# Hybrid decoder step on one core: norm scales applied at evacuations, router scaled by token, sample attention in column tiles

## The chip, the core and the metric

The kernel runs on one core of a Trainium2 chip. The metric is device time in microseconds; lower is better. Engines: TensorE (PE), VectorE (DVE), ScalarE (ACT), GpSimd (POOL) and the DMA queues that SyncE (SP) and GpSimd issue to. The engines run their own instruction queues in order and wait for each other on semaphores.

## What is computed

One step of a two-layer decoder for 264 tokens: 256 of a prompt, and 8 of a sample group with 256 past positions each. Width 1024, all in float32. Cut to what matters:

```
h = rmsnorm(x, norm_mix[0]);  z = gelu(h @ w_in);  u, v = split(z);  v = layernorm(v)
x = x + (u * (W_s v + b)) @ w_out                    # chunked mixer
h = rmsnorm(x, norm_ffn[0]);  x = x + (silu(h @ wg) * (h @ wu)) @ wd
kv = rmsnorm(x, kv_norm) @ w_kv;  h = rmsnorm(x, norm_mix[1])
q, gates = h @ b_w_in;  x = x + (gated compressed + selected + window attention) @ b_w_out
h = rmsnorm(x, norm_ffn[1]);  x = x + top-2-of-8 expert SwiGLU(h)
y = rmsnorm(x, norm_final)
```

rmsnorm(x, g) is x * rsqrt(mean(x * x) + eps) * g for each token.

## The kernel before, in words

Activations lie transposed: channels on partitions (8 chunks of 128, `KC`), the 264 tokens (`NT`) along the free axis. To keep float32 accuracy, each operand is split in two fp32r halves: ACT casts it (`_hi`), DVE subtracts the cast from the original (`_lo`, the rest), and PE adds up hi*hi, hi*lo and lo*hi. One **item** is 128 output columns of a dense weight; its product (`product`, L1370) is 24 matmuls of 264 columns into one of four banks `B[0..3]` (18 for the last part of the down stage). Items come in the stages vu (16), ao (8), gu (44), dn (24), kv (12), q (8), bo (8). SP loads four items as a 2 MB tile of a two-slot ring (L434); ACT casts (`round_to`, L568, L576), DVE takes the rest (`rest_to`, L892, L897), into three buffers `d_hi`, `d_lo`. The order of each engine's queue is written out by hand: `round_to(stage, c)` and `rest_to(stage, c)` run up to two items ahead of product c, and they stand between the other work of that engine.

A norm before: ACT squares x (L564, L587), DVE adds the chunks up (`add_up`, L858), PE multiplies by a matrix of 1/1024 (`mean_of`, L1362), ACT takes the root (`std`, L557, with a table load), DVE the reciprocal (`inv_std`, L853). Only then `split_normed` (L877, L883, L887) and `round_normed` (L579) scale and split x, chunk by chunk, and the products of the next stage start. Evacuations: gelu, silu, the copy to `kvT` and half of `Q` on ACT (L596, L600, L631, L645, L652), products and residual additions on DVE (L982, L958), other half of `Q` on DVE (L1011). In the kv stage DVE also copies the new keys to `X2` (L1001), while POOL clears `Q` (L492 to L494). The mask of the mixer's matrix is applied by DVE (L912).

Sample attention: `sample_scores` (L1504) adds 16 matmuls of 256 columns into one bank for each of two key sets, with queries `Qz` zero outside their sample's rows (L1509). The values are 32 matmuls with 16 output rows, one sample each (L1594); their rows are copied out (L717, L1130) and turned back by 16 small matmuls (L1605). Then follow the 16 heads of the prompt: scores, softmax, turning, weighing.

Router: norm of x, `normed(late("ffn1"))` (L1156), 8 matmuls (L1625), a copy (L740), transposes of tokens and logits (L1631, L1636), then a chain of small DVE operations (L1174 on). POOL zeroes `slot_rows` and `out_rows` in DRAM (L481 to L484) and scatters token rows there. Eight expert blocks follow in this execution (L1690 on). SP loads their first 11 MB as soon as the heads are done.

Of the kernel before, what the change touches and what calls it, by code (L numbers as in the profile page):

```python
# [21 lines left out]
F32 = mybir.dt.float32  # L22
# [6 lines left out]
P = 128  # L29
# [104 lines left out]
def build(nc, xT, wd, moe, vectors, params, late_in, spatial, spatial_bias, consts, cmp_pages, k_pages, v_pages, win_k, win_v, state_win, page_table,  # L134
          y_out, v_out, kv_out, past_out):
    with ExitStack() as ctx:
# [15 lines left out]
        zeros = sb("zeros", [P, 256])  # L152

# [36 lines left out]
        win_v_past = sbd("win_v_past", [P, SLOT])  # L190
        sq3 = slc_v[:, 0:KC * NT].rearrange("p (k t) -> p k t", t=NT)
# [21 lines left out]
        b_s = carve(8, NT)  # L213

# [5 lines left out]
        orow = arena[0:NH, qz_at:qz_at + NS * 2 * P]  # L220
# [86 lines left out]
        x_in = sem("x_in")  # L307
# [49 lines left out]
        zeros_ready, rows_zeroed, slots_ready, early_ready = sem("zeros_ready"), sem("rows_zeroed"), sem("slots_ready"), sem("early_ready")  # L357
        sel_ready, tok_zero = sem("sel_ready"), sem("tok_zero")
# [44 lines left out]
        def _(sp):  # L403
            sp.dma_start(x[:], xT).then_inc(x_in, 16)
            sp.dma_start(VE[:], vectors).then_inc(setup_in, 16)
            wn = 0
# [4 lines left out]
            for n, t in enumerate(TILES):  # L411
# [21 lines left out]
                else:  # L433
                    sp.dma_start(ring[:, n % NSLOT, :], wd[wn]).then_inc(done, 16)  # L434
# [31 lines left out]
            for half in range(2):  # L466
                sp.wait_ge(h_ready, 44 + 4 * half)
                sp.dma_start(y_out[:, 4 * half:4 * half + 4, :], hB[:, 4 * half:4 * half + 4, :]).then_inc(y_stored, 16)
# [6 lines left out]
        def _(pool):  # L475
            nc.gpsimd.memset(zeros[:], 0.0).then_inc(zeros_ready, 1)
            pool.wait_ge(vn_ready, 8)
            pool.dma_start(v_out, vT).then_inc(v_stored, 16)
            pool.dma_start(past_out, state_win).then_inc(past_stored, 16)
            pool.wait_ge(zeros_ready, 1)  # L480
            for rows in (slot_rows.rearrange("b p n -> (b p n)"), out_rows[0:NO_ROW, :].rearrange("r n -> (r n)")):  # L481
                rows = rows.rearrange("(p q n) -> p q n", p=P, n=256)
                pool.dma_start(rows, zeros[:].unsqueeze(1).to_broadcast(list(rows.shape))).then_inc(rows_zeroed, 16)
            pool.dma_start(out_rows[NO_ROW:NO_ROW + 1, :].rearrange("o (q n) -> (o q) n", n=256), zeros[0:4, :]).then_inc(rows_zeroed, 16)  # L484
# [22 lines left out]
            pool.dma_start(grow[:], gsam[0:NS, :]).then_inc(grow_in, 16)  # L507

# [39 lines left out]
        def _(act):  # L548
# [8 lines left out]
            def std(n, eps):  # L557

                act.wait_ge(mean_done, n)
                nc.scalar.activation(rstd[:, :], STAT[:, 0:NT], ACT.Sqrt, bias=vector("eps")[:, eps:eps + 1]).then_inc(std_ready, 1)  # L560

            def squares(norm, k, dst=hB):
# [1304 lines left out]
```

## Time and profile before

| | us |
|---|---|
| three runs | 1375.67, 1376.95, 1380.04 |
| median | 1376.95 |
| the profiled execution, device time | 1382.43 |
| its span | 1380.8 |
| PE busy / DVE / ACT / POOL | 1306.5 / 1055.2 / 920.7 / 73.0 |

The profile is of one execution. The dense stages end near 388 us, the sample attention near 468, the heads near 546, the output projection at 570, the routing near 595; the expert blocks last to 1363. Matmuls are pipelined, so the duration of one is longer than its step to the next.

### The profile page before, as it was taken

How to read it: one execution, taken by the hardware profiler on the slowest of the kernel's cores; microseconds unless marked ns; L12 is line 12 of the kernel's file. 1: busy time of each engine (PE TensorE's matmuls, PEld its weight loads, DVE VectorE, ACT ScalarE, POOL GpSimd, SP SyncE). 2: the span in 40 equal slices, each digit the busy share in tenths (PEclk: the TensorE clock that was granted, in tenths of full speed). 3: DMA queues.
4: the chain of work that ended last, by engine and by line, in shares of the span. 5: the costliest groups of instructions: out<-in, count | busy, mean ns of one | idle time of the engine just before them, and what ended most of it. 6: DMA issues, size and time to landing. Idle time of an engine off the chain costs nothing.

```text
span 1380.8 us, 21526 instructions
## 1 busy us (share of the span) xinstructions
PE 1306.5 (95%) x7292; PEld 1109.1 (80%) x7292; DVE 1055.2 (76%) x1539; ACT 920.7 (67%) x1353; POOL 73.0 (5%) x74
## 2 busy tenths in 40 slices
PE   4998999996998999899999999999999999999996
PEld 4988999996966677678888888888788888887874
DVE  5776555458423487689899899898998998998985
ACT  5535444445372287478798788887987987887863
POOL 0010000004200000020000000000000000002500
PEclk9999999998998999999999999999999999999998
DMA  8399544455565001679999899899998998998930
GB/s 328 130 379 402 187 180 181 177 197 175 187 218 187 1 1 48 288 299 421 363 392 409 318 419 396 332 417 370 352 413 326 404 406 323 416 394 320 408 146 32
DMA packets 59280, 391.50 MB, mean 284 GB/s; under 512 B 6639, under 2 KB 12915, under 8 KB 20627
## 3 DMA queue, kind: packets, MB, share of 16 engines
q1 hardware_dynamic: 50578, 354.29, 65.2%
q0 software_dynamic: 8640, 36.40, 7.2%
q8 instruction: 38, 0.62, 0.2%
q14 instruction: 24, 0.19, 0.0%
HBM read 367.41 MB, written 27.45 MB: 286 GB/s over the span
## 4 chain that ended last, share of the span: by engine, by line
PE 84%; DVE 9%; ACT 3%; issue 3%; DMA 0%; ACTq 0%; DVEq 0%
PE bank L1710 16%; PE bank L1712 16%; PE bank L1711 16%; PE bank L1381 8%; PE bank L1382 8%; PE bank L1383 8%; DVE w_lo L1263 2%; PE bank L1695 1%; PE bank L1509 1%; PE bank L1594 1%; PE bank L1567 1%; ACT w_hi L756 1%; DVE rstd L856 1%; ACT arena L662 1%; PE bank L1555 1%
## 5 line engine op out<-in xcount | busy, mean ns | idle before, releaser
L1263 DVE TENSOR_TENSOR w_lo<-raw,w_hi 128x1024 fp32r<-128x1024 f32 x528 | 623.2, 1218 | 37.1 <-ACT w_hi L756 19.7
L756 ACT CAST w_hi<-raw 128x1024 fp32r<-128x1024 f32 x528 | 543.0, 1055 | 95.3 <-PE bank L1712 94.4
L1710 PE MATMUL bank<-w_hi,xg_hi 128*128 128x512 f32 x704 | 275.2, 391 | 1.4 <-DVE w_lo L1263 1.4
L1712 PE MATMUL bank<-w_hi,xg_lo 128*128 128x512 f32 x704 | 274.3, 390 | 0.0
L1711 PE MATMUL bank<-w_lo,xg_hi 128*128 128x512 f32 x704 | 273.9, 389 | 0.0
L897 DVE TENSOR_TENSOR d_lo<-ring,d_hi 128x1024 fp32r<-128x1024 f32 x120 | 146.6, 1223 | 102.6 <-ACT d_hi L576 102.4
L1381 PE MATMUL bank<-hA_hi,d_hi 128*128 128x264 f32 x640 | 187.9, 294 | 21.1 <-DVE hA_lo L887 15.2
L1382 PE MATMUL bank<-hA_lo,d_hi 128*128 128x264 f32 x640 | 185.3, 289 | 0.0
L1383 PE MATMUL bank<-hA_hi,d_lo 128*128 128x264 f32 x640 | 184.9, 289 | 0.0
L576 ACT CAST d_hi<-ring 128x1024 fp32r<-128x1024 f32 x120 | 125.4, 1046 | 58.5 <-PE bank L1383 55.0
L1710 PEld LDWEIGHTS bank<-w_hi,xg_hi 128*128 128x128 f32 x704 | 132.3, 188 | 29.3 <-DVE w_lo L1263 2.1
L1712 PEld LDWEIGHTS bank<-w_hi,xg_lo 128*128 128x128 f32 x704 | 132.1, 188 | 27.8
L1711 PEld LDWEIGHTS bank<-w_lo,xg_hi 128*128 128x128 f32 x704 | 132.2, 188 | 27.3
L1710 PE MATMUL bank<-w_hi,hm_hi 128*128 128x512 f32 x352 | 148.2, 421 | 1.9 <-DVE w_lo L1263 0.6
L1381 PEld LDWEIGHTS bank<-hA_hi,d_hi 128*128 128x128 f32 x640 | 123.9, 194 | 23.7 <-issue 20.6
L1712 PE MATMUL bank<-w_hi,hm_lo 128*128 128x512 f32 x352 | 139.4, 396 | 0.0
L1711 PE MATMUL bank<-w_lo,hm_hi 128*128 128x512 f32 x352 | 138.5, 393 | 0.0
L1382 PEld LDWEIGHTS bank<-hA_lo,d_hi 128*128 128x128 f32 x640 | 124.8, 195 | 0.1
L1383 PEld LDWEIGHTS bank<-hA_hi,d_lo 128*128 128x128 f32 x640 | 124.0, 194 | 0.0
L1710 PEld LDWEIGHTS bank<-w_hi,hm_hi 128*128 128x128 f32 x352 | 66.6, 189 | 19.5 <-DVE w_lo L1263 8.5
L1712 PEld LDWEIGHTS bank<-w_hi,hm_lo 128*128 128x128 f32 x352 | 66.6, 189 | 15.9
L1711 PEld LDWEIGHTS bank<-w_lo,hm_hi 128*128 128x128 f32 x352 | 67.1, 191 | 11.6
(320 smaller groups left out, 1611.0 us busy)
## 6 DMA issues: line engine op xcount, KB each, us to landing
raw<-in_moe SPq DMA_DIRECT2D x264, 1024.0 KB, 6.8
ring<-in_wd SPq DMA_DIRECT2D x30, 2048.0 KB, 8.5
out_rows<-zeros POOLq DMA_DIRECT2D x1, 6656.0 KB, 62.1
slot_rows<-zeros POOLq DMA_DIRECT2D x1, 6144.0 KB, 44.9
out_rows<-yrow POOLq DMA_DIRECT2D x8, 512.0 KB, 7.8
xs<-slot_rows POOLq DMA_DIRECT2D x7, 512.0 KB, 3.6
arena<-in_cmp_pages POOLq DMA_DIRECT2D x16, 128.0 KB, 2.5
X2v<-in_cmp_pages POOLq DMA_DIRECT2D x16, 128.0 KB, 2.8
```

Source lines behind the costliest of these rows:

```text
L576: nc.scalar.copy(d_hi[:, n % NDS, :], raw_item(n)).then_inc(d_hi_ready, 1)
L662: nc.scalar.copy(lines[:, n % NLINE, :], X2[v][:, m:8 * SEGS:8]).then_inc(line_ready, 1)
L756: nc.scalar.copy(w_hi[:, i % NSPLIT, :], raw[:, u % NRAW, ITEM * (i % 2):ITEM * (i % 2) + ITEM])\
L856: settle(V.reciprocal(rstd[:, :], rstd[:, :]))
L897: V.tensor_tensor(d_lo[:, n % NDS, :], raw_item(n), d_hi[:, n % NDS, :].bitcast(F32), ALU.subtract)\
L1263: V.tensor_tensor(w_lo[:, i % NSPLIT, :], raw[:, (i // 2) % NRAW, ITEM * (i % 2):ITEM * (i % 2) + ITEM], w_hi[:, i % NSPLIT, :].bitcast(F3 ...
L1381: T.matmul(out, w_hi_[:, j, :], hi[:, k, :], start=(first and j == 0), stop=False)
L1382: T.matmul(out, w_hi_[:, j, :], lo[:, k, :], start=False, stop=False)
L1383: i = T.matmul(out, w_lo_[:, j, :], hi[:, k, :], start=False, stop=(last and k == ks[-1]))
L1710: T.matmul(out, lhs_hi, hi, start=first, stop=False)
L1711: T.matmul(out, lhs_hi, lo, start=False, stop=False)
L1712: return T.matmul(out, lhs_lo, hi, start=False, stop=last)
```

## The change

The token scale of a norm is no longer applied to x. ACT rounds x times the norm's weight (`round_weighted`) as each chunk of x is ready, DVE takes its rest, the products start at once, and the reciprocal root multiplies each product at its evacuation, on DVE (`scaled`, `u_scale`, the gate, up and query scalings). ACT then applies gelu and silu in SBUF. Means stand one or two products into the next stage; `root_table` loads the root's table ahead of time. At the start SP loads vectors, one item and x in halves:

```diff
-            sp.dma_start(x[:], xT).then_inc(x_in, 16)
             sp.dma_start(VE[:], vectors).then_inc(setup_in, 16)
+            sp.dma_start(ring[:, 0, 0:DITEM], wd[0][:, 0:DITEM]).then_inc(item_in[0], 16)
+            for half in range(2):
+                sp.dma_start(x[:, 4 * half:4 * half + 4, :], xT[:, 4 * half:4 * half + 4, :]).then_inc(x_in[half], 16)
+            sp.wait_ge(item_in[0], 16)
+            sp.dma_start(ring[:, 0, DITEM:2 * DITEM], wd[0][:, DITEM:2 * DITEM]).then_inc(item_in[1], 16)
...
+                    first = 2 * DITEM if n == 0 else 0
+                    sp.dma_start(ring[:, n % NSLOT, first:], wd[wn][:, first:]).then_inc(done, 16)
```

POOL applies the mask of the mixer, and zeroes the DRAM rows only after the gates are stored:

```diff
+            pool.wait_ge(spatial_in, 48)
+            nc.gpsimd.tensor_tensor(wsT[:], w_s, const("upto").unsqueeze(1).to_broadcast([P, 8, P]), ALU.mult).then_inc(ws_ready, 1)
+            nc.gpsimd.tensor_tensor(dg[0:NS], ident[0:NS, 0:NS].unsqueeze(1).to_broadcast([NS, 8, NS]),
+                                    vector("w00")[0:NS, :].unsqueeze(2).to_broadcast([NS, 8, NS]), ALU.mult).then_inc(ws_ready, 1)
...
+            pool.wait_ge(zeros_ready, 1)
+            for rows in (slot_rows.rearrange("b p n -> (b p n)"), out_rows[0:NO_ROW, :].rearrange("r n -> (r n)")):
+                rows = rows.rearrange("(p q n) -> p q n", p=P, n=256)
+                pool.dma_start(rows, zeros[:].unsqueeze(1).to_broadcast(list(rows.shape))).then_inc(rows_zeroed, 16)
```

ACT (in the kv stage it also copies the new keys, `new_keys`, after item 7 and at the start of q):

```diff
+            def root_table():
+
+                nc.scalar.activation(warm[0:1, 0:1], zeros[0:1, 0:1], ACT.Sqrt)
...
+            def round_weighted(weight, k, dst, ready):
+
+                nc.scalar.activation(dst[:, k, :], x[:, k, :], ACT.Copy, scale=weight[:, k:k + 1]).then_inc(ready, 1)
...
+            act.wait_ge(zeros_ready, 1)
+            root_table()
+            act.wait_ge(setup_in, 16)
+            round_to("vu", -2)
             for k in range(KC):
-                nc.scalar.activation(hB[:, k, :], x[:, k, :], ACT.Square).then_inc(sq_ready, 1)
-            act.wait_ge(setup_in, 16)
+                if k % 4 == 0:
+                    act.wait_ge(x_in[k // 4], 16)
+                round_weighted(vector("mix0"), k, hA_hi, h_hi_ready)
+            round_to("vu", -1)
...
+                nc.scalar.activation(sqr[:, k, :], x[:, k, :], ACT.Square).then_inc(sq_ready, 1)
+            round_to("vu", 1)
             std(1, 0)
...
-                projected(act, "vu", c)
-                nc.scalar.activation(vT[:, c, :], B[c % 4][:, 0:NT], ACT.Gelu_apprx_tanh).then_inc(v_ready, 1)
+                act.wait_ge(v_scaled, c + 1)
+                nc.scalar.activation(vT[:, c, :], vT[:, c, :], ACT.Gelu_apprx_tanh).then_inc(v_ready, 1)
...
+                if c == 3:
+                    std(3, 1, ln_rstd)
...
+                    for k in range(KC):
+                        act.wait_ge(ln_scaled, k + 1)
+                        nc.scalar.activation(vT[:, k, :], vT[:, k, :], ACT.Identity, bias=vector("lnb")[:, k:k + 1]).then_inc(vn_ready, 1)
...
+            root_table()
             for c in range(KC):
                 round_to("ao", c)
+                act.wait_ge(x_ready, c + 1)
+                round_weighted(vector("ffn0"), c, hA_hi, h_hi_ready)
                 squares(1, c)
+            round_to("gu", 1)
             std(4, 0)
...
-                nc.scalar.activation(sil[:, f % 2, :], B[2 * (f % 2)][:, 0:NT], ACT.Silu).then_inc(sil_ready, 1)
+                act.wait_ge(gate_scaled, f + 1)
+                nc.scalar.activation(sil[:, f % 2, :], sil[:, f % 2, :], ACT.Silu).then_inc(sil_ready, 1)
...
                 round_to("dn", 12 * (c // 4) + 8 + c % 4)
+                act.wait_ge(x_ready, KC + c + 1)
+                round_weighted(vector("kvn"), c, hA_hi, h_hi_ready)
...
+                round_weighted(vector("mix1"), c, hC_hi, q_hi_ready)
...
+                if c < KC:
+                    round_weighted(vector("mix1"), c, hB, gate_in)
+                if c == 7:
+                    new_keys(0)
...
+                if c == 0:
+                    projected(act, "kv", 11)
+                    new_keys(1)
+            act.wait_ge(gp_scaled, 1)
+            nc.scalar.activation(gT[0:48, :], gT[0:48, :], ACT.Sigmoid, bias=par("bgate")[0:48, :]).then_inc(sig_ready, 1)
...
+            act.wait_ge(orow_done, 1)
+            nc.scalar.copy(orow[:, :], B[0][:, :]).then_inc(orow_ready, 1)
...
+            root_table()
             for c in range(KC):
                 round_to("bo", c)
+                act.wait_ge(x_ready, 16 + c + 1)
+                nc.scalar.activation(hB[:, c, :], x[:, c, :], ACT.Copy, scale=late("ffn1")[:, c:c + 1]).then_inc(weighted, 1)
...
+            act.wait_ge(mean_done, 6)
+            nc.scalar.activation(tok_rstd[:, 0:2], STAT[:, 0:2], ACT.Sqrt, bias=vector("eps")[:, 0:1])
```

DVE (its copies of new keys, `split_normed`, the mask, and the copies of value rows are gone):

```diff
+            def rest_weighted(weight, k, hi, lo, which):
...
+                dve.wait_ge(hi_done, nrest[which])
+                V.scalar_tensor_tensor(lo[:, k, :], x[:, k, :], weight[:, k:k + 1], hi[:, k, :].bitcast(F32), ALU.mult, ALU.subtract)\
+                    .then_inc(lo_done, 1)
...
+            dve.wait_ge(setup_in, 16)
+            rest_to("vu", -2)
             for k in range(KC):
-                add_up(hB, k, sq_ready, k + 1)
-            dve.wait_ge(setup_in, 16)
+                rest_weighted(vector("mix0"), k, hA_hi, hA_lo, 0)
+            rest_to("vu", -1)
+            for k in range(KC):
+                add_up(sqr, k, sq_ready, k + 1)
+            rest_to("vu", 1)
...
+            def scaled(to, stage, c, ready):
+                projected(dve, stage, c)
+                V.tensor_tensor(to, B[c % 4][:, 0:NT], rstd[:, :], ALU.mult).then_inc(ready, 1)
...
-                add_up(vT, k, v_ready, k + 1)
+                scaled(vT[:, k, :], "vu", k, v_scaled)
+                if k:
+                    add_up(vT, k - 1, v_ready, k)
+            add_up(vT, KC - 1, v_ready, KC)
...
+            u_scale(0)
+            u_scale(1)
...
+                if k == 4:
+                    u_scale(2)
...
+            u_scale(3)
+            rest_to("vu", 11)
+            inv_std(ln_rstd)
             for k in range(KC):
                 if k == 5:
...
+                    u_scale(4)
+                V.scalar_tensor_tensor(vT[:, k, :], vT[:, k, :], vector("lng")[:, k:k + 1], ln_rstd[:, :], ALU.mult, ALU.mult)\
...
+            rest_to("vu", 13)
+            u_scale(5)
+            u_scale(6)
+            u_scale(7)
...
+                for r in rests:
+                    rest_weighted(vector(r[0]), c, *r[1:])
...
+                if f >= 2:
+                    dve.wait_ge(hF_ready, f - 1)
+                V.tensor_tensor(sil[:, f % 2, :], B[2 * (f % 2)][:, 0:NT], rstd[:, :], ALU.mult).then_inc(gate_scaled, 1)
...
+                V.tensor_tensor(hB[:, f % 4, :], B[2 * (f % 2) + 1][:, 0:NT], rstd[:, :], ALU.mult).then_inc(up_scaled, 1)
...
+            for c in range(12):
+                rest_to("kv", c)
+                scaled(kvT[:, c, :], "kv", c, kv_ready)
...
+                for odd, done in ((0, q_even), (1, q_odd)):
+                    rows = slice(64 * odd, 64 * odd + 64)
+                    V.scalar_tensor_tensor(Q[half:half + 64, 2 * c + odd, :], B[c % 4][rows, 0:NT], HD ** -0.5, rstd[rows, :],
+                                           ALU.mult, ALU.mult).then_inc(done, 1)
...
+                i = V.scalar_tensor_tensor(col(0, t)[0:r, :], MISC[0:r, 8 * t:8 * t + 8], tok_rstd[0:r, t:t + 1], b_router[0:r, :],
+                                           ALU.mult, ALU.add)
```

PE (sample scores and values in four column tiles; each group of 32 rows holds two samples; router matmuls between the output products; the mean there is one column per token group):

```diff
+                    pe.wait_ge(v_scaled, c - 3)
...
+                    pe.wait_ge(u_scaled, c - 11)
                 product(B[c % 4], hA_hi, hA_lo, each=chunks_of(h_ready, 0) if c == 0 else None)
+                if c == 1:
+                    mean_of()
                 if c == 8:
                     mean_of()
-                if c == 12:
+                if c == 11:
...
+                if f == 0:
+                    mean_of()
...
                 if c < 4:
-                    pe.wait_ge(x_ready, 16)
+                    pe.wait_ge(x_ready, 13 + c)
...
+                if c == 1:
+                    mean_of()
+            pe.wait_ge(q_lo_ready, 8)
+            pe.wait_ge(gate_in, 8)
...
-                for j in range(16):
-                    i = T.matmul(B[n][:, 0:PAST], Qz[:, j % 2, j // 2, :], keys[:, j // 2, j % 2, :], start=(j == 0), stop=(j == 15))
+                for j in range(4):
+                    for g in range(4):
+                        b, rows_ = 2 * g + j // 2, slice(32 * g, 32 * g + 32)
+                        i = T.matmul(B[n][rows_, 0:PAST], Qz[:, j % 2, b, rows_], keys[:, b, j % 2, :], start=(j == 0), stop=(j == 3))
...
-            for b in range(NS):
-                out = B[b // 2][0:NH, 256 * (b % 2):256 * (b % 2) + 256]
+            for half in range(2):
                 for j in range(4):
-                    i = T.matmul(out, PTs[:, j, b * NH:(b + 1) * NH], vals[j // 2][:, b, j % 2, :], start=(j == 0), stop=(j == 3))
-                if b % 2:
-                    i.then_inc(orow_done, 1)
+                    for g in range(4):
+                        rows_ = slice(32 * g, 32 * g + 32)
+                        i = T.matmul(B[0][rows_, 256 * half:256 * half + 256], PTs[:, j, rows_], vals[j // 2][:, 2 * g + half, j % 2, :],
+                                     start=(j == 0), stop=(j == 3))
+            i.then_inc(orow_done, 1)
...
+                    pe.wait_ge(orow_ready, 1)
+                for half in range(2):
+                    T.matmul(by_half(rows_, half), orow[:, 256 * half + c * P:256 * half + c * P + P], by_half(ident, half),
...
+                if c >= 2:
+                    logits(c - 2)
+            logits(KC - 2)
+            logits(KC - 1)
...
+            turn_tokens(0, 0)
+            pe.wait_ge(sum_step, 42)
             for t, (a, z) in enumerate(spans):
+                i = T.matmul(STAT[0:z - a, t:t + 1], total[:, a:z], mean[:, 0:1], start=True, stop=True)
+            i.then_inc(mean_done, 1)
+            nmean[0] += 1
+            pe.wait_ge(lT_ready, 1)
```

## Rows read from the trace of the kernel before

**Rows 1.** Page: the chain that ended last, by engine.

```profile
PE 84%; DVE 9%; ACT 3%; issue 3%; DMA 0%; ACTq 0%; DVEq 0%
```

**Rows 2.** Busy time by stretch: length; PE, PEld, DVE, ACT, POOL; clock, DMA share, GB/s.

```profile
390.00:470.00 80.00, 73.96 (x326) 50.98 (x327) 18.49 (x69) 30.43 (x57) 0.64 (x1) 0.86 0.40 140
470.00:546.00 76.00, 73.32 (x477) 56.90 (x476) 62.51 (x247) 60.45 (x224) 0.00 (x0) 0.99 0.01 1
...
780.00:1250.00 470.00, 469.05 (x2122) 382.90 (x2121) 427.64 (x449) 388.47 (x469) 4.83 (x9) 1.00 0.95 378
```

**Rows 3.** Instruction groups by line; busy, mean ns, then idle before and its releaser.

```profile
L897 DVE TENSOR_TENSOR d_lo<-ring,d_hi 128x1024 fp32r<-128x1024 f32 x120 | 146.6, 1223 | 102.6 <-ACT d_hi L576 102.4
...
L576 ACT CAST d_hi<-ring 128x1024 fp32r<-128x1024 f32 x120 | 125.4, 1046 | 58.5 <-PE bank L1383 55.0 <-DMA ring<-in_wd 3.4
...
L958 DVE TENSOR_TENSOR x<-x,bank 128x264 f32<-128x264 f32 x24 | 10.3, 429 | 25.1 <-PE bank L1383 25.1
```

**Rows 4.** Chain in order of time, start: start us, us, what.

```profile
0.98 5.09 DMA x<-in_x
...
13.92 1.81 DVE rstd L856
...
18.68 0.56 PE bank L1381
```

**Rows 5.** Timeline, seams up to gate/up: start us, us, what, idle before and releaser.

```profile
71.13 1.06 PE L1411 MATMUL bank<-consts_sb,arena 128*128 128x128 f32 x8 [0.33 <-DVE arena L937]
...
105.58 0.43 DVE L958 TENSOR_TENSOR x<-x,bank 128x264 f32<-128x264 f32 x1 [0.99 <-PE bank L1383]
...
108.48 0.43 DVE L958 TENSOR_TENSOR x<-x,bank 128x264 f32<-128x264 f32 x1 [0.85 <-PE bank L1383]
...
123.71 0.43 DVE L982 TENSOR_TENSOR hB<-sil,bank 128x264 f32<-128x264 f32 x1 [0.32 <-PE bank L1383]
```

**Rows 6.** Timeline, down to key/value.

```profile
310.73 0.43 DVE L958 TENSOR_TENSOR x<-x,bank 128x264 f32<-128x264 f32 x1 [0.28 <-PE bank L1383]
...
330.09 5.98 DVE L1001 COPY arena<-arena 64x128 f32<-64x128 f32 x1
...
340.90 0.38 ACT L645 COPY arena<-bank 128x264 f32<-128x264 f32 x1 [2.98 <-PE bank L1383]
```

**Rows 7.** Timeline, PE ahead of the compression products.

```profile
390.52 0.53 PE L1473 MATMUL bank<-consts_sb,arena 48*128 48x48 f32 x3 [2.27 <-ACT arena L654]
...
393.68 1.91 PE L1489 MATMUL bank<-arena,params_sb 128*128 128x512 f32 x2
...
398.62 1.04 PE L1489 MATMUL bank<-arena,params_sb 128*128 128x512 f32 x2
```

**Rows 8.** Chain, sample attention.

```profile
414.72 7.10 PE bank L1509 x32
424.41 8.78 PE bank L1509 x32
...
445.60 15.28 PE bank L1594 x64
...
467.36 0.61 PE bank L1607 x2
```

**Rows 9.** Timeline, DVE at the router.

```profile
570.19 0.43 DVE L958 TENSOR_TENSOR x<-x,bank 128x264 f32<-128x264 f32 x1 [1.55 <-PE bank L1383]
...
581.69 0.17 DVE L1174 TENSOR_TENSOR lg<-bank,late_sb 128x16 f32<-128x16 f32 x1 [2.15 <-PE bank L1636]
```

**Rows 10.** Timeline, SP issues the last of the value loads.

```profile
413.81 0.43 SPq L432 DMA_DIRECT2D win_v_past<-in_win_v  x1
```

**Rows 11.** Page: DMA issues; KB each, median us from issue to landing.

```profile
ring<-in_wd SPq DMA_DIRECT2D x30, 2048.0 KB, 8.5
out_rows<-zeros POOLq DMA_DIRECT2D x1, 6656.0 KB, 62.1
```

**Rows 12.** DMA issues from 60 to 140 us.

```profile
ring<-in_wd SPq DMA_DIRECT2D x5, 2048.0 KB, 11.1
```

More of the change, by code:

```diff
@@ L555, in settle, with std, squares @@
                 act.wait_ge(act_step, nstep[0])
[L557 removed]
+            def std(n, eps, dst=rstd):
                 act.wait_ge(mean_done, n)
[L560 to L562 removed]
+                nc.scalar.activation(dst[:, :], STAT[:, 0:NT], ACT.Sqrt, bias=vector("eps")[:, eps:eps + 1]).then_inc(std_ready, 1)
+            def squares(norm, k, dst=sqr):
                 act.wait_ge(x_ready, 8 * norm + k - 7)
@@ L571, in round_to @@
                     n = rounded[0]
-                    if n % 4 == 0:
+                    if n < 2:
+                        act.wait_ge(item_in[n], 16)
+                    elif n == 2 or n % 4 == 0:
                         arrived(act, WTILES[n // 4])
@@ L714, in _ @@
             exp_head(1)
-            for j in (0, 2):
-                act.wait_ge(orow_done, j + 1)
-                nc.scalar.copy(orow[:, 512 * j:512 * j + 512], B[j][0:NH, :]).then_inc(orow_ready, 1)
+            act.wait_ge(orow_done, 1)
+            nc.scalar.copy(orow[:, :], B[0][:, :]).then_inc(orow_ready, 1)
             for h in range(NH):
@@ L746, in _ @@
                     act.wait_ge(ht_done, 2 * t + half + 1)
-                    nc.scalar.copy(htok[0:r, t, 512 * half:512 * half + 512], HT[2 * t + half][0:r, :]).then_inc(ht_ready, 1)
+                    nc.scalar.activation(htok[0:r, t, 512 * half:512 * half + 512], HT[2 * t + half][0:r, :], ACT.Copy,
+                                         scale=tok_rstd[0:r, t:t + 1]).then_inc(ht_ready, 1)
             act.wait_ge(rank_in, 1)
@@ L953, in _, with add_chunk @@
                         .then_inc(gated_lo, 1)
-            def add_chunk(c, norm, stage, item, squared=hB):
+            def add_chunk(c, norm, stage, item, squared=sqr, rests=()):
                 rest_to(stage, item - 1)
@@ L1446, in _ @@
                             pe.wait_ge(hF_lo_ready, ks[-1] + 1)
-                        if part == 0 and half == 0 and j < 2:
-                            pe.wait_ge(hF_ready, FC)
+                        if part == 0 and half == 0:
+                            pe.wait_ge(hF_ready, FC - 1 if j < 2 else FC)
                         product(B[j], hF_hi, hF_lo, ks, part == 0, part == 2)
-            mean_of()
             for c in range(12):
                 if c < 4:
-                    pe.wait_ge(x_ready, 16)
+                    pe.wait_ge(x_ready, 13 + c)
                 if c >= 4:
@@ L1602, in _ @@
                 if c == 0:
-                    pe.wait_ge(orow_ready, 4)
-                for b in range(NS):
-                    T.matmul(rows_[:, b * NH:(b + 1) * NH], orow[:, 256 * b + c * P:256 * b + c * P + P], ident[0:NH, 0:NH],
+                    pe.wait_ge(orow_ready, 1)
+                for half in range(2):
+                    T.matmul(by_half(rows_, half), orow[:, 256 * half + c * P:256 * half + c * P + P], by_half(ident, half),
                              start=False, stop=False, skip_group_check=True)
@@ L1615, in _, with logits @@
             weigh(NH - 1)
+            def logits(k):
+                pe.wait_ge(weighted, k + 1)
+                i = T.matmul(MISC[0:NE, 0:NT], w_router[:, k, :], hB[:, k, :], start=(k == 0), stop=(k == KC - 1))
+                if k == KC - 1:
+                    i.then_inc(lT_done, 1)
             for c in range(KC):
```

191 lines of the change are left out of this document (78 added, 113 removed).

## The prediction

> **What bounds the kernel now.** I read the chain of waits first: it lies 84% on TensorE (PE) and 9% on VectorE (DVE) [rows 1]. Then the busy time by stretch [rows 2]: in the expert blocks PE is busy 469.05 of 470 us at full clock. The change leaves their code alone, so I take nothing from them. From 390 to 470 us the mean granted clock is only 0.86: part of that stretch runs at 1.2 instead of 2.4 GHz. So the change can act at four places: the start, the seams between dense stages, the sample attention, and the router. I price each on the profiled execution (span 1380.8 us, device time 1382.43). The median of the runs shown is 1376.95, 5.48 below it, and I subtract the same gain from the median.
>
> **Prices.** A 1024-column cast on ScalarE (ACT) takes 1.05 us, its rest on DVE 1.22, a 264-column DVE operation that reads a bank 0.43 [rows 3]. The trace has no scaling at an evacuation; the last of these is the nearest row, and I take it for each new scaling and each weighted rounding or rest (bounds 0.35, what back-to-back ones leave, and 0.6). Back to back, operations start some 0.07 earlier than their durations say.
>
> **Start and first projection.** Now x lands at 6.07, the reciprocal takes 1.81 from 13.92, and the first product starts at 18.68 [rows 4]. After: vectors, one weight item and half of x (1.1 MB together, like x alone now) land near 6.3, so the product starts near 7.8, 11 us earlier. It is not kept. Squares, mean, root and reciprocal now follow the second product (ending near 16, its chunks at 1.2 GHz at first), so the first scaling comes at 20 and the fifth product near 23. From there a loop is formed: scaling on DVE, gelu on ACT, ACT's next cast, DVE's next rest, next scaling. Its steps 0.36 + 0.31 + 0.97 + 1.14, with some 0.2 of handovers, are 3.0 us against the 2.90 at which PE takes a product, from the addition to x at 105.58 to the one at 108.48 [rows 5]. In the LayerNorm more DVE and ACT work stands ahead of the rests: u scalings between sums, and the bias additions, now on ACT, ahead of the cast for the last product. Following the three queues step by step I get PE waits of 1.4, 1.9, 1.1, 1.5 and 2.6 us, 8.5 together. The mask moved to GpSimd frees 1.2 us on DVE, but may hold DVE's two-input rests. The v transposes start near 70 instead of 71.13 [rows 5]: gain 1, bounds -4 (all waits longer by half) and +5 (half of them absent).
>
> **Output projection to gate/up.** Now the last x addition starts at 108.48, and the second gate/up product ends just before 123.71 [rows 5]. That is 15.2 us, of which two products are 5.8. After, the split of x is made chunk by chunk beside the products (0.43 more on ACT and on DVE of 2.90 us, covered). Only a mean of 0.33 stands between the two products, and root and reciprocal hide behind the next ones, since four banks are free. Gain 9.1. Per gate/up pair DVE rises from about 3.3 to 4.2 us of 5.8: still covered. The start of the down product no longer waits for the last multiply: 0.9, less 0.4 of new waits in the short down items (two weighted rests per chunk): 0.5.
>
> **Down to key/value.** The last addition starts at 310.73, the fifth product of the stage ends at 340.90 [rows 6]: 30.2 us, with two splits in the gap and one DVE copy of 5.98 us beside a GpSimd memset. After: five products of 2.90, a mean, 0.5 waiting at the first and 1.7 at the second product (rests queued behind x additions), together 17.1. The eight copies per half move to ACT (0.25 each, in its 1.4 us of slack per item). Gain 13.1.
>
> **Before the attention.** PE waits 2.27 us for the sigmoid and its table load, then runs its first line product in 1.91 us for two records, later pairs in 1.04 [rows 7]. The sigmoid goes ahead of the last query product, three line copies are ready, and PE has no gap before them: gain 2.3 + 1.8 = 4.1.
>
> **Sample attention in column tiles.** Scores: 32 records in 7.10 us, and 32 in 8.78 (its beginning at half clock). Values: 64 records in 15.28 us at 16 output columns, 0.239 a record, no cheaper than 128 columns at 0.222 [rows 8]. So time follows the 256 streamed columns, and a record leaves most of the array unused; the count of streams is unchanged. Bounds: serial, gain 0; four groups fully side by side, a quarter. I take a third, near the quarter, since the rows show the array's width idle. Scores: 4.7, and 4.3 at the half clock, which I let stand: 9.0. Values: 5.6, some of it at 1.2 GHz, instead of 15.3: 9.7. The Trainium skill (TensorE: Matmul & The Clock Gate, Measured speedup vs the span model) reports 2.38 times for three column tiles; at that efficiency four would give 3.2 times and a sum 0.6 us larger; no row here shows tiles. The part behind the values ends at 467.97 [rows 8], 7.1 us after them: sixteen turning matmuls become four, and the one bank copy hides behind the two matmuls ahead of them. With 12 records of some 0.22 and the copy's hand-over 7.1 becomes 3.4: gain 3.7 in either case.
>
> **Router.** The last x addition starts at 570.19, and DVE reads the logits at 581.69 [rows 9]: 11.5 us for mean, table load, root, reciprocal, eight weightings and eight router matmuls in a row. After: six router matmuls lie inside the output products (12 records of 0.22, +2.7 there), the table is loaded early, and the root is of three columns. What is left is an estimate from like rows: addition 0.4, weighting and square 0.8, sum 0.4, one-column means 0.7, roots 0.4, reciprocals 0.3, route transposes 0.4, hand-overs 0.5, together 3.9. 11.5 becomes 6.6; ACT's scaled token copies delay the exponential by 0.2 at the end: gain 4.7.
>
> **Sum:** 1 + 9.1 + 0.5 + 13.1 + 4.1 + 9.0 + 9.7 + 3.7 + 4.7 = 54.9. 1382.43 becomes 1327.5; the median 1376.95 becomes 1322.
>
> **Rivals.** (a) The column tiles run one after another. For: nothing in this trace shows two matmul streams overlapping, and at 16 columns none did (all in one column group). The gain falls by 18.7 to 36.2: 1341. The skill has the reason on the same page (What overlaps and what doesn't): weights are loaded beside running matmuls only if row groups differ, and these tiles share theirs. The trace does not bear that out for whole-array loads: PE is busy 469.05 of 470 us with a load before every matmul, all in one row group [rows 2].
> (b) The zeroing of the slot and output rows (6.6 and 6.1 MB) moves from 72 us to about 392, into the loads of the value pages, the last of which is issued at 413.81 [rows 10] and lands near 422. Now the zeroing lands after 62.1 us beside weight loads [rows 11], and ring loads of 2 MB, 8.5 us at the median, take 11.1 in that stretch [rows 11, 12]. If value loads lose half their rate, they land near 452, 20 us after PE now wants them (432); if they lose a third and SP's issue stays the limit, nothing waits. Middle: 12 us lost, 1334.
> (c) Slower: with PE mostly idle in the shortened sample part, the clock stays at 1.2 GHz through the 16 heads, where it is 0.99 now and PE is busy 73.3 of 76 us [rows 2]. A head, 76 us by 16 or 4.8 us, would take up to 4.8 more; from 12 heads on the gain is gone, and with all 16 it is 1399. Against: after the present half-clock stretch the full clock comes back before the heads.
> (d) The change does not do what it says at the first projection: GpSimd's mask multiply holds DVE's rests. The Trainium skill (SBUF — State Buffer, Who interferes with whom) says that a DVE instruction with two SBUF inputs contends with a GpSimd instruction that reads SBUF; no row of this trace has such a pair. The multiply happens once and costs one such multiply, 2 to 5 us: 1326, inside the forecast's range.
>
> **Numbers.** Chances: forecast with (d) 0.67, (a) 0.18, (b) 0.11, (c) 0.04. The forecast's own range is 1313 to 1331, from the bounds of the first projection (5 down, 4 up), full side-by-side streams (2.5) and the clock. The range given reaches to (a) and (b): 1312 to 1343. A difference under 0.3% (4.1 us) cannot be told from no change. Only (c), or several misses at once, reaches that: faster 0.95, same 0.02, slower 0.03.
>
> **What would show it.** First dense product near 8 us, v transposes near 70; no PE gap over 1 us before the gate/up stage; key/value seam 13 us shorter; table load for the sigmoid ahead of the last query product; records of different column groups starting under 0.1 us apart in the sample scores; logits on DVE about 6.6 us after the last output product; expert blocks unchanged. PE waiting for value pages would show (b), a clock under 0.9 in the heads (c). I am wrong if the seams keep waits, or if the first projection takes longer by more than its start gains.

## The result, and the profile after

The changed kernel takes 1343.22 us (median of four runs, 1341.46 to 1346.57), the kernel before 1377.87 in the same comparison: ratio 0.9749, interval 0.973 to 0.9768. The gain is 34.7 us, clearly a gain, but the forecast was 54.9 (1322), and the result lies just outside its range (1312 to 1343). The profiled execution took 1342.47 us, span 1340.7.

First the chain that ended last, by engine (page). Against [rows 1] PE falls from 84% to 76%. SyncE's issuing (SPq) and DMAs, which held nothing, now hold 5%:

```profile
PE 76%; DVE 10%; issue 5%; ACT 4%; SPq 3%; DMA 2%; DVEq 0%; ACTq 0%
```

Busy time by stretch, columns as in [rows 2]. The heads lie from 433 to 511 us now and run at full clock, and the expert blocks are as busy as before:

```profile
390.00:470.00 80.00, 61.97 (x455) 46.14 (x453) 43.74 (x172) 39.09 (x145) 0.00 (x0) 0.89 0.58 232
434.00:511.00 77.00, 73.20 (x483) 56.54 (x482) 64.09 (x253) 60.68 (x225) 0.00 (x0) 1.00 0.02 6
780.00:1250.00 470.00, 468.42 (x2120) 382.62 (x2120) 428.62 (x463) 385.58 (x467) 22.85 (x14) 1.00 0.95 377
```

Instruction groups, as [rows 3]. The new scaling at an evacuation (L967) costs 0.43, as assumed; a weighted rounding (L605) 0.51 and its rest (L940) 0.49, a little more than the 0.43 assumed:

```profile
L950 DVE TENSOR_TENSOR d_lo<-ring,d_hi 128x1024 fp32r<-128x1024 f32 x120 | 146.0, 1223 | 88.0 <-ACT d_hi L596 87.9
...
L967 DVE TENSOR_TENSOR arena<-bank,rstd 128x264 f32<-128x264 f32 x28 | 11.6, 427 | 8.4 <-PE bank L1453 8.2
L605 ACT ACTIVATE hA_hi<-x,vectors_sb 128x264 fp32r<-128x264 f32 x24 | 11.6, 512 | 13.3 <-DVE x L1023 12.9 <-DMA x<-in_x 0.3
L940 DVE SCALAR_TENSOR_TENSOR hA_lo<-x,vectors_sb,hA_hi 128x264 fp32r<-128x264 f32 x24 | 11.1, 486 | 1.2 <-ACT hA_hi L605 1.2
```

Then the timeline at the places the forecast named (start, duration, what, idle before and its releaser). The v transposes start at 73.34; before they started at 71.13 [rows 5]. The second gate/up product and the fifth key/value product end near 117.0 and 321.2, where they ended before 123.7 and 340.9 [rows 5, 6]. PE waits 12.90 us for the window's values; the logits reach DVE 3.6 us after the last addition to x (537.94), not 11.5 [rows 9]:

```profile
73.34 1.04 PE L1481 MATMUL bank<-consts_sb,arena 128*128 128x128 f32 x8
...
321.25 0.43 DVE L967 TENSOR_TENSOR arena<-bank,rstd 128x264 f32<-128x264 f32 x1 [0.59 <-PE bank L1453]
...
372.25 0.60 PE L1557 MATMUL bank<-consts_sb,arena 128*8 128x128 f32 x4 [2.33 <-DVE arena L1099]
372.51 2.26 POOL L524 DMA_DIRECT2D slot_rows<-zeros  x1
...
374.02 2.00 PE L1566 MATMUL bank<-arena,params_sb 128*128 128x512 f32 x2
...
393.65 1.93 PE L1588 MATMUL bank<-ring,arena 128*32 128x256 f32 x32
...
401.57 0.87 SPq L445 DMA_DIRECT2D win_v_past<-in_win_v  x1
...
422.90 1.51 PE L1674 MATMUL bank<-slc_v,arena 128*32 128x256 f32 x12 [12.90 <-DMA win_v_past<-in_win_v]
...
541.53 0.48 DVE L1244 SCALAR_TENSOR_TENSOR lg<-bank,tok_rstd,late_sb 128x8 f32<-128x8 f32 x3
```

Laid stretch by stretch over the profile of before, the two traces give this account (us gained):

| stretch | forecast | traces |
|---|---|---|
| start to the v transposes | +1 | -2.2 |
| to the third gate/up product | 9.1 | 8.9 |
| gate/up and down | 0.5 | 0.1 |
| down to key/value | 13.1 | 12.9 |
| last query product to the first sample score | 4.1 | 1.4 |
| sample scores to the first value product | 9.0 | 1.7 |
| values | 9.7 | 9.1 |
| turning back | 3.7 | 3.5 |
| heads | 0 | 0.7 |
| output projection and routing | 4.7 | 2.4 |
| expert blocks and end | 0 | 1.7 |

That is 40.2 between two profiled executions. The one of before was 4.6 us above its median, the one of after 0.8 below; less these, 34.8 is left, the measured gain. Four rows miss by more than 2: the scores' (7.3), the start (3.2), the seam before the attention (2.7) and the router (2.3).

### The profile page after: what moved, and what is told of

The parts are those of the page before. It is cut to its first block, busy times and chain, and to the rows that moved or that the text cites. A ratio compares the mean times of both kernels' runs of the same rounds, so it can differ in the third digit from the quotient of the medians.

```text
span 1340.7 us, 21550 instructions
## 1 busy us (share of the span) xinstructions
PE 1272.4 (95%) x7272; PEld 1082.5 (81%) x7272; DVE 1053.5 (79%) x1552; ACT 929.6 (69%) x1378; POOL 76.0 (6%) x76
## 4 chain that ended last, share of the span: by engine, by line
PE 76%; DVE 10%; issue 5%; ACT 4%; SPq 3%; DMA 2%; DVEq 0%; ACTq 0%
PE bank L1809 16%; PE bank L1811 16%; PE bank L1810 16%; PE bank L1451 7%; PE bank L1452 6%; PE bank L1453 6%; DVE w_lo L1333 3%; SPq L422 2%; DMA win_v_past<-in_win_v 2%; DVE d_lo L950 2%; PE bank L1794 1%; PE bank L1646 1%; ACT w_hi L812 1%; ACT d_hi L596 1%; DMA ring<-in_wd 1%
## 5 line engine op out<-in xcount | busy, mean ns | idle before, releaser
L1452 PEld LDWEIGHTS bank<-hA_lo,d_hi 128*128 128x128 f32 x640 | 121.9, 191 | 0.1
L1453 PEld LDWEIGHTS bank<-hA_hi,d_lo 128*128 128x128 f32 x640 | 121.3, 190 | 0.0
L1810 PEld LDWEIGHTS bank<-w_lo,hm_hi 128*128 128x128 f32 x352 | 66.9, 190 | 11.5
```

What stands on the lines that cost most here:

```text
L1452: T.matmul(out, w_hi_[:, j, :], lo[:, k, :], start=False, stop=False)
L1453: i = T.matmul(out, w_lo_[:, j, :], hi[:, k, :], start=False, stop=(last and k == ks[-1]))
L1810: T.matmul(out, lhs_hi, lo, start=False, stop=False)
```

## The experiments

Theory A was formed on the DMA view of 340 to 480 us (KB each, median us to landing). A load of a value page takes 14.4 us and that of the window's values 21.2, beside 12.8 MB of zeroing. The second fence has the same two loads in the kernel before:

```profile
out_rows<-zeros POOLq DMA_DIRECT2D x1, 6656.0 KB, 60.5
slot_rows<-zeros POOLq DMA_DIRECT2D x1, 6144.0 KB, 29.5
...
slc_v<-in_v_pages SPq DMA_DIRECT2D x16, 128.0 KB, 14.4
win_v_past<-in_win_v SPq DMA_DIRECT2D x1, 2048.0 KB, 21.2
```

```profile
slc_v<-in_v_pages SPq DMA_DIRECT2D x16, 128.0 KB, 2.3
win_v_past<-in_win_v SPq DMA_DIRECT2D x1, 2048.0 KB, 8.5
```

The timeline adds that not only the flights got longer. SyncE now takes 25.7 us to issue the sixteen page loads, where it took 17.2, so the last load leaves some 8 us later. The DMA share, the mean busy share of the 16 DMA engines, is 1.01 from 376.5 to 400 us, where it was 0.69 in the kernel before (398 to 422): they were full. The issues in the changed kernel, then in the kernel before:

```profile
375.81 25.72 SPq L443 DMA_DIRECT2D slc_v<-in_v_pages  x16
```

```profile
396.53 17.24 SPq L430 DMA_DIRECT2D slc_v<-in_v_pages  x16
```

**1. Zeroing after the value loads.**

```diff
             pool.dma_start(grow[:], gsam[0:NS, :]).then_inc(grow_in, 16)
+            pool.wait_ge(past_v_in, 16 * (NS * PAGES + 1))
             pool.wait_ge(zeros_ready, 1)
```

> The changed kernel with one wait more: GpSimd issues the zeroing of the slot and output rows only when all value pages and the window's values have landed (near 410 us). Theory A (the zeroing takes the bandwidth of the value pages, which land at 422.9 although TensorE wants them at 413.3): the value products start near 413.5 instead of 422.9, run nearer to full clock (4 to 6 us instead of 6.2), 1331 us, a gain of 9.5 to 12. Rival B (the pages are late because SyncE issues them late and slowly; the last leaves at 400.1 in any case): the values still land after 418 us and the gain is under 5 us. Rival C: the zeroing, now beside the heads and ending near 475, delays the output projection's or the experts' weights and gives part back; then the wait ahead of the values is gone but the total stays above 1337.

1332.46 us, ratio 0.967 (0.9656 to 0.9683). The page loads are issued in 17.2 us again, the last load leaves at 392.90 in place of 401.57 and lands 8.8 us later. PE waits only for DVE's copies and starts the values at 414.56. The values still take 6.6 us, at clock 0.55, so this part of the expectation missed. Theory A holds. Rival B falls with its premise: SyncE issued late because of the zeroing itself. C falls too.

**2. Zeroing early, as before.** The five lines move back behind the store of `v_out`.

> The changed kernel with the zeroing put back where the kernel before has it, right behind the store of the mixer's values (near 67 us). Theory A: the same gain at the values as with the late zeroing, 9.5 to 12 us, but the zeroing now lies beside the weight loads of the output projection and gate/up stages, which have 1.5 us to spare per item: 0 to 2 us lost there; 1331 to 1334. Rival B: under 5 us gained.

1331.93 us, ratio 0.9666 (0.9652 to 0.9681): the same gain, with nothing lost beside the weight loads, though the ring loads from 60 to 140 us now take 12.4 us (8.3 in the changed kernel). The same two rows as above, in this kernel:

```profile
slc_v<-in_v_pages SPq DMA_DIRECT2D x16, 128.0 KB, 2.4
win_v_past<-in_win_v SPq DMA_DIRECT2D x1, 2048.0 KB, 8.7
```

The later experiments on the changed kernel stand on this one, called E below, where nothing else is said.

**3. The mask on VectorE.** On the changed kernel; the multiply moves from GpSimd's queue to DVE's, behind `u_scale(6)`.

> The changed kernel with the mask of the mixer's matrix multiplied by VectorE again, in its idle 4 us before the last u scaling, instead of by GpSimd at 24.7 us. Theory D (GpSimd's multiply holds VectorE: the first copying addition at 25.12 takes 2.30 us instead of 0.43): that addition takes 0.43, the sixth product starts 0.5 to 1.9 us earlier, and 0.5 to 1.9 us are gained in all: 1341.5 to 1342.7. Rival E (the wait at 27 us comes from the loop of scaling, gelu, cast and rest that fills after the first reciprocal, not from GpSimd): no difference.

1343.4 us, ratio 0.9748: no difference from the change. The mechanism is in the trace: in the changed kernel DVE's addition of two SBUF tiles starts at 25.12 and ends at 27.42, with GpSimd's multiply (24.71 to 27.13), while a scaling from a bank at 24.78 took its 0.42 beside it. Without the multiply the addition takes 0.42. So theory D is right in its place, where the sixth product's gap of 0.63 is gone, and too small to be measured in the whole. First the changed kernel, then experiment 3:

```profile
24.71 2.42 POOL L492 TENSOR_TENSOR arena<-arena,consts_sb 128x1024 f32<-128x1024 f32 x1 [23.42 <-DMA arena<-in_spatial_bias]
...
25.12 2.30 DVE L922 TENSOR_TENSOR total<-arena 128x264 f32<-128x264 f32 x1
```

```profile
25.24 0.42 DVE L918 TENSOR_TENSOR total<-arena 128x264 f32<-128x264 f32 x1
```

**4. Column tiles, one group after the other.** On the kernel of experiment 1, only the order of the loops:

```diff
-                for j in range(4):
-                    for g in range(4):
+                for g in range(4):
+                    for j in range(4):
```

> The kernel of the late zeroing with the same column tiles and the same number of matmuls, only in another order: all matmuls of one column group in a row, then the next group, in the scores and in the values. Theory F (streams of different column groups run side by side only if they stand next to each other in TensorE's queue): each score set goes from 1.93 to about 7.1 us, the values from 4 to 6 us to 14 or 15; 19 to 20 us more than the late zeroing, some of the first set's hidden by nothing: near 1350. Rival G (the width of a tile alone makes a matmul cheap, whatever its neighbours are): the same times as the late zeroing, within 1 us.

1341.24 us, ratio 0.9738 (0.9721 to 0.9755): 8.8 above experiment 1. Neither theory's sizes hold. Windows over the first score set (32 records and a few others) and the values (64):

```profile
395.70:400.40 4.70, 4.70 (x35) 2.53 (x35) 1.33 (x6) 2.03 (x2) 0.00 (x0) 1.00 1.02 364
420.20:428.40 8.20, 8.16 (x65) 4.57 (x65) 0.00 (x0) 1.35 (x8) 0.00 (x0) 1.00 1.02 407
```

A record costs 0.143 in the scores (4.59 by 32), where it was 0.222 with full width [rows 8] and is 0.060 with neighbours of other groups (1.93 by 32). The starts of the single records in the traces say why. Within one group they stand 0.216 us apart, as they do at full width, so a narrow record is no cheaper by itself and rival G is out. But the first record of the next group starts at 396.640, beside the fifth of the eight before it (396.635): two groups run side by side for half of their records. In experiment 1 the records of all four groups start within 0.02 us (393.645 to 393.665), and the next four 0.24 later. So the whole gain of the tiles comes from groups running side by side, and the order decides how many do: theory F is right in kind, and wrong only in leaving no overlap where two groups meet. In the values 8.16 us at full clock stand against 6.6 at half clock (3.7 at full clock in experiment 6): there the clock takes most of what the order gives.

From the first score to the last value the two traces differ by 5.2 us. Another 2.4 lie before the third product of the first stage, which the edit does not touch, so the 8.8 between the medians is not all the order's.

**5. The kernel before with column tiles alone.** The loops of scores, values and turning back, and one bank copy by ACT, from the change.

> The kernel before with one part of the change alone: the sample scores, the values and the turning back in column tiles (the zeroing stays early, as it is there). By the changed kernel's trace the two score sets should take 1.93 us each instead of 7.10 and 8.78, the values 5 to 6.2 at half clock instead of 15.3, the turning 3.5 instead of 7.1: 24 to 25 us in all, near 1353. Rival: part of it is given back, because TensorE, now idle for more of the stretch, works at 1.2 GHz in the transposes, scores and heads beside it: 18 to 21 us, 1356 to 1359.

1357.26 us, ratio 0.9849 (0.9834 to 0.9864): 20.6 us gained, the rival's 18 to 21, not 24 to 25. The half clock moved in as the rival said: the second score set took 2.9 us, the values 5.35 (from the chain of waits):

```profile
416.57 2.86 PE bank L1507 x32
...
433.57 5.35 PE bank L1593 x64
```

**6. Waits filled with matmuls** (on E):

```diff
+            def filler(n):
+                for _ in range(n):
+                    T.matmul(STAT[:, 0:256], ident, kvT[:, 0, 0:256], start=True, stop=True)
+            filler(6)
             pe.wait_ge(vp_ready, 3)
...
+            filler(6)
             pe.wait_ge(spt_ready, 1)
```

> The kernel of the early zeroing with six matmuls of 256 columns more, which nobody reads, in each of the two places where TensorE waits in the sample attention (for the maxima of the sample scores, 2.7 us, and for the copies of the turned probabilities, 2.8 us). Theory H (these idle stretches are what the granted clock falls after, and the half clock lengthens the turning, the first head's scores, the values and the turning back): clock 1.0 in them, values in 3.9 us instead of 5.05, 3 to 5 us gained, 1327 to 1329. Rival I (the clock falls by something else, or the added matmuls end later than the waits they fill): no gain, or 1 us lost.

1328.66 us, ratio 0.9641 (0.9625 to 0.9657), 3.3 us under E. The window over the values: 65 records in 3.7 us at clock 1.0. E needed 5.05 at 0.72, the changed kernel 6.2 at 0.59. One row each of this kernel, of E, and of the changed kernel (its wait, then its values):

```profile
412.20:416.00 3.80, 3.71 (x65) 2.09 (x66) 0.03 (x1) 1.44 (x8) 0.00 (x0) 1.00 0.01 4
```

```profile
413.30:418.40 5.10, 5.05 (x65) 2.44 (x65) 0.00 (x0) 1.37 (x8) 0.00 (x0) 0.72 0.01 3
```

```profile
414.00:422.90 8.90, 0.00 (x1) 0.03 (x2) 0.00 (x0) 0.53 (x4) 0.00 (x0) 0.52 1.03 431
422.90:429.10 6.20, 6.20 (x65) 3.20 (x66) 0.00 (x0) 0.00 (x0) 0.00 (x0) 0.59 1.01 425
```

Theory H holds for this stretch. The two intervals overlap slightly, but from the first score to the last value the traces differ by 3.4 us, about as much as the medians. The clock has a share of chance too: at the first line products, ahead of any filling, it fell in E (371.8) and stayed at 1.0 here, behind the same wait of 2.33 us.

**7. The cast ahead of the bias additions** (on E):

```diff
-                round_to("vu", KC + c)
+                round_to("vu", KC + c + (c == 4))
...
-                if k == 5:
+                if k == 3:
                     rest_to("vu", 12)
+                if k == 5:
                     u_scale(4)
```

> The kernel of the early zeroing with ScalarE's cast for the last u product ahead of its eight bias additions of the LayerNorm, and VectorE's rest for the product before it two scalings earlier. Theory J (the wait of 3.1 us ahead of the last product of the first projection comes from the bias additions, which stand ahead of the cast in ScalarE's queue): that wait goes from 3.1 to under 0.5, the one before it from 1.3 to under 0.5, 3 to 4 us gained, 1328 to 1329. Rival K (the last product then only waits for its bank's u scaling, or the v transposes wait for the bias additions in its place): the same wait appears later, under 1 us gained.

1326.81 us, ratio 0.9623 (0.9606 to 0.964), 5.1 us under E. The wait of 3.10 ahead of the last product becomes 0.34, the one before 0.48 in place of 1.28. In the changed kernel, then here:

```profile
63.12 3.34 ACT L639 ACTIVATE arena<-arena,vectors_sb 128x264 f32<-128x264 f32 x8
...
67.44 1.23 DVE L950 TENSOR_TENSOR d_lo<-ring,d_hi 128x1024 fp32r<-128x1024 f32 x1 [3.47 <-ACT d_hi L596]
...
68.81 0.36 PE L1451 MATMUL bank<-hA_hi,d_hi 128*128 128x264 f32 x1 [3.10 <-DVE d_lo L950]
```

```profile
64.67 0.36 PE L1452 MATMUL bank<-hA_hi,d_hi 128*128 128x264 f32 x1 [0.34 <-DVE d_lo L950]
```

Theory J holds. It gives more than the waits, since the last product, which ran mostly at half clock, takes 3.16 us instead of 4.70.

**8. The router's matmuls behind the output products** (on E): `logits(c - 2)` leaves the loop, `for c in range(KC): logits(c)` follows it.

> The kernel of the early zeroing with all eight router matmuls behind the last output product, six of which stood between the products. In the changed kernel each of the six costs 0.62 us there, and in a row it costs 0.44. Theory L (they are serial work on TensorE in either place, dearer in between): the output products take 2.90 us each again, 3.7 us less, the row costs 2.7 more, 1 to 1.8 us gained: 1330 to 1331. Rival M (what stands between the products hides better): 1 to 2 us lost, because the router's matmuls now follow the last addition.

1331.03 us, ratio 0.9659 (0.9644 to 0.9673). From the first output product to the first expert product the trace has 43.3 us, 45.0 in E; 0.9 in the medians is not told apart from nothing. So theory L is borne out by the trace alone, and rival M falls.

**9. The kernel before with the zeroing moved alone.**

> The kernel before with the zeroing alone moved to the place the change gives it, behind the gates (near 392 us). Theory A' (the zeroing costs time only because the rest of the change has made TensorE want the values 30 us sooner): the last value load leaves at 413.8 and lands some 21 us later, near 435, while TensorE wants the values at 445.6; nothing or up to 2 us lost, 1377 to 1380. Rival N (the place costs the same 11 us in any kernel): near 1389.

1382.9 us (12 runs), ratio 1.0024 (1.0012 to 1.0037): 3 to 4 us lost, more than theory A' had and far from rival N. The load of the window's values leaves at 419.77, not 413.81, and takes 25.2 us, so its lateness shows even in this kernel:

```profile
445.10 1.87 PE L1594 MATMUL bank<-slc_v,arena 128*16 128x256 f32 x4 [8.01 <-DMA win_v_past<-in_win_v]
```

PE waits 8.01 us, of which 2.83 were there before.

**10 to 12. Mends together.** 10: E with 6, 7 and 8. 11: also 3, and three filling matmuls at each of two waits in the routing. 12: also five where PE waits for L1099's copies.

> Four mends together: early zeroing, the filling matmuls of the sample attention, the cast ahead of the bias additions, the router's matmuls behind the output products. By the single runs' differences to the early zeroing (3.3, 5.1 and 0.9 us) 1322 to 1324 if they add up; 1325 or more if they share a wait.

> The four mends, the mask on VectorE in its idle time, and three filling matmuls in each of the two places of the routing where TensorE waits (for the ranks' input and for the copies of token rows). If the half clock there costs 1.2 us or more in the matmuls that gather the first block's rows, as their 8.25 us against 7.08 in the kernel before say: 1 to 3 us less than the four mends alone. If the filling only moves the fall of the clock: no difference within 1 us.

> The same and five filling matmuls where TensorE waits 2.3 us for the copies of turned prompt values, ahead of the compression products. If that wait is what lets the clock fall for the first pairs of line products (2.0 us for two records instead of 1.04), the first line product to the first sample score takes 19.5 us or less instead of 21.0: 1 to 1.5 us less than without them. Rival: ScalarE's line copies (1.12 us a piece) bound these products, and full clock only makes TensorE wait for them: no difference.

1321.47 (ratio 0.9581, 0.9559 to 0.9604), 1321.36 (0.9593, 0.9571 to 0.9615) and 1320.21 us (0.9571, 0.9551 to 0.9591). The mends of 10 add up. The three kernels can't be told apart. In 11's trace the clock stays at 1.0 from 372 to 1280 us, where 10's falls once around 415 and once around 528; but the gathering matmuls take 7.07 us in both, so nothing was left to gain there. In 12 the stretch from the first line product to the first score takes 19.3 us, as expected, against 21.0 in 11. That is no proof: experiment 6 shows 19.3 without this filling. The second score set then takes 2.8 us instead of 1.93, for the clock falls at 391 in place of 369. All three are 22 to 23 us faster than the change.

## Why the prediction was wrong

**What failed first: "if they lose a third and SP's issue stays the limit, nothing waits".** The zeroing beside the value loads was rival (b), with a chance of 0.11, and the sum put it at nothing. By the forecast's own terms PE came to the values 13 us sooner after their loads (4.1 and 9.0), and 12.8 MB of zeroing started under these loads, yet the gain of the scores was taken in full. The runs show both halves of the step wrong. The load of the window's values took 2.5 times as long (8.5 to 21.2 us), that of a page six times (2.3 to 14.4). And SyncE's issue did not stay as it was: it stretched from 17.2 to 25.7 us. Moving the zeroing back gives 11.3 us (experiment 2). Rival (b)'s own price, 12, came close, though it was only a middle between 20 and nothing. The zeroing's place was right as well, apart from the start: the gates are stored sooner too, so it began at 372.5, not 392.

**Start and first projection: forecast +1, measured -2.2.** The start was right within a microsecond (first product 8.78, not 7.8), and so was the loop: the products from the sixth on stand 3.00 us apart. Two steps failed. The fifth product starts at 25.0, not near 23: the trace has waits of 0.61, 1.52, 0.40 and 0.63 there, which the forecast hardly had. And the sum "PE waits of 1.4, 1.9, 1.1, 1.5 and 2.6 us" is 9.2 instead of 8.5 (1.38, 1.52, 1.96, 1.27 and 3.10). The last product's half clock adds 1.5. The result lies inside the bounds, -4 and +5, but the forecast's own sign of being wrong came true: from the first product to the transposes it takes 12.1 us more (64.6 for 52.5), and the start gained 9.9. That the mask holds DVE (d) was right, at 1.9 us on DVE and 0.6 on PE.

**The two dense seams: right.** 8.9 and 12.9 for 9.1 and 13.1. What hides the second scalings and rests is PE's 2.90 us an item, as assumed.

**Before the attention: forecast 4.1, measured 1.4.** "three line copies are ready, and PE has no gap before them" failed: the sigmoid's wait is gone, but PE waits 2.33 us for DVE's copies of turned prompt values (L1099), which stand behind DVE's query scalings. The clock falls again in the line products (2.00 us for two records at 374.02). The 1.8 us priced for it were partly a chance of the profiled execution: in experiment 9, whose code is the same there as before, line products to first score take 19.3 us, not 21.0, and in experiment 6 the clock stayed full behind the same 2.33. No run moves these copies, so what the wait costs by itself stays open.

**Column tiles: right in mechanism and nearly in size.** Forecast 22.4 in all, measured alone 20.6 (experiment 5). The sets run at a quarter (1.93 us), better than the third that was taken, and the values at a third to 0.4 because their clock is half. Rival (a), serial tiles, is out: the weight loads, all of one row group, did not keep the streams apart, and the records of different groups start under 0.1 us apart, as the forecast asked for. The Trainium skill (TensorE: Matmul & The Clock Gate, The mechanism, what overlaps and what doesn't) says that a weight load overlaps with running matmuls only when the row groups differ; read strictly, that would have left no gain, and the measurement decides against it. The Trainium skill (same page, Measured speedup vs the span model) has 2.38 times for three tiles; the 3.2 times that the forecast estimated from it for four were bettered, by 3.7 times in the first score set (7.10 to 1.93).

**Router: forecast 4.7, measured 2.4.** From the last addition to the logits 3.6 us, forecast 3.9 (6.6 less the 2.7 inside the products). But the six matmuls between products cost 3.7, not 2.7; the exponential comes 0.8 later behind ACT's scaled copies, not 0.2; and the gathering matmuls from 548.23 on take 8.25 us, mostly at half clock, instead of 7.08. This last part is in part chance: in E they take 7.25.

**Clock: rival (c) is out** (heads at 1.00), but it had the right question. In the changed kernel the half clock took part of the probabilities' turning, of the values and of the routing. In E it did reach the first heads, from 423.0 to 429.8 us, and cost 0.7 us there (82.4 us from the last value to the output projection, 81.7 in the changed kernel); it did not stay.

**The arithmetic of the reference.** The sum was made against a profiled execution 4.6 us above its median. Between the last query product and the first score that execution has 2.7 us more than those of experiments 5 and 9, whose code is the same there: 5.4 to the first line product where they have 4.4, and 21.0 from there where they have 19.3. A gain counted there is probably not one from the median. If the parts add up, the gain of E, 45.3, is 20.6 of tiles (experiment 5) and 24.7 of the rest, for which the forecast had 32.5. So of the 20 us between 54.9 and the measured 34.7, 11.3 were lost to the zeroing, 7.8 in the rest and 1.8 in the tiles; these make 20.9, for E was compared with other executions of the kernel before.

## What to carry to other kernels

When a change makes an engine want data sooner, price every transfer on that path again at its new neighbours, and bulk transfers that nobody waits for (a zeroing, a store) go where no load is due: the same DMA, moved from its early place to the value loads, cost 3 to 4 us in the slower kernel and 11 in the faster one. Shortened TensorE work between waits may meet the half clock: the values took 6.2 us and not 3.7. Price it so, or fill the waits. In hand-written queue orders look for short work that waits for many steps (eight bias additions) ahead of a cast that PE needs.

## What the runs showed of the hardware

- Matmuls of 32 output columns and 256 streamed ones cost 0.060 us a record if neighbours in the queue go to different column groups, 0.143 if the groups come one after the other, against 0.222 at full width. The streams are not shorter: in every order the records of one group start 0.216 us apart at full clock.
- Six filling matmuls in each of two waits of 2.5 and 2.8 us kept the granted clock at 1.0 from 400 to 419 us; without them, in E, its mean was 0.64 from 402 to 416. Later fillings changed where the clock fell, or kept it from falling, but no time that could be measured.
- Two writes of 6.1 and 6.7 MB from one small tile slowed 128 KB loads from 2.3 to 14.4 us and a 2 MB load from 8.5 to 21.2, and stretched the issue of sixteen loads from 17.2 to 25.7.
- A DVE addition of two SBUF tiles took 2.30 us beside a GpSimd multiply that reads SBUF, and 0.42 without it; a scaling from a bank kept its 0.42 beside the same multiply. The Trainium skill (SBUF — State Buffer, Who interferes with whom) says that GpSimd's reads hold DVE's instructions with two SBUF inputs, and the trace agrees.
